# Who makes the low parts of the gated outputs, and when the split of the next weights runs, in a two-block transformer kernel

## What is computed

```python
# first block, layer 0: attention A (windowed), layer 1: attention B
h = h + (o * silu(z)) @ w_out                 # o: attention output, z: gate
gate = sigmoid(rms_norm(h, g) @ ple_w_gate)
h = h + (p @ ple_w) * gate
# second block: a state-space branch and attention C over the same input
y_ssm = ssd_branch(...)
y_att = softmax(q k^T * scale + f_i - f_j, causal) @ v * silu(z_att)
g_ssm, g_att = split(sigmoid(g_logit + b_gate))
merged = g_ssm * (y_ssm @ w_proj_ssm) + g_att * (y_att @ w_proj_att)
x = x + gate * (merged @ w_out)
return rms_norm(x, final_norm_w)
```

## Time and profile before

| | before |
|---|---|
| median of 3 runs | 2878.92 us (2878.53 to 2882.49) |
| the profiled execution's own time | 2878.6 us |
| its span in the trace | 2877.3 us |
| TensorE busy | 2767.1 us, 96% of the span |
| VectorE busy | 1551.6 us, 54% |
| ScalarE busy | 1353.7 us, 47% |
| GpSimd busy | 895.3 us, 31% |
| mean granted TensorE clock | 0.99 of full |
| DMA | 148.78 MB, mean 52 GB/s |

### The profile page before, as it was taken

One profiled execution on the slowest core, in us unless ns is written; L12 is line 12 of the kernel. 1 busy time (PEld: TensorE's weight loads), 2 busy tenths in 40 slices (PEclk: granted clock), 3 DMA queues, 4 the chain that ended last, 5 costly groups with the idle time before them and its releaser, 6 DMA issues.

```text
span 2877.3 us, 36420 instructions
## 1 busy us (share of the span) xinstructions
PE 2767.1 (96%) x13800; PEld 2268.0 (79%) x13800; DVE 1551.6 (54%) x2706; ACT 1353.7 (47%) x2485; POOL 895.3 (31%) x728
## 2 busy tenths in 40 slices
PE   8999989999999999999998999999999999999997
PEld 6778867777788888887775877778787888887875
DVE  6667774643388888886468866521003444433034
ACT  5658864335376766674435344531123334333122
POOL 0334441223365555653122222033221111112331
PEclk9999999999999999999999999999999999999999
DMA  3111131221100000003110310032211010011232
GB/s 132 38 33 41 37 130 64 87 77 44 34 10 10 10 10 10 10 30 132 59 60 28 110 30 19 27 117 73 67 44 37 30 30 30 26 32 47 73 117 73
DMA packets 54444, 148.78 MB, mean 52 GB/s; under 512 B 6144, under 2 KB 14976, under 8 KB 54272
## 3 DMA queue, kind: packets, MB, share of 16 engines
q1 hardware_dynamic: 54272, 146.46, 15.6%
HBM read 129.66 MB, written 16.78 MB: 51 GB/s over the span
## 4 chain that ended last, share of the span: by engine, by line
PE 86%; DVE 5%; ACT 4%; POOL 2%; issue 2%; DMA 0%; SPq 0%; ACTq 0%; POOLq 0%; DVEq 0%
PE ps L327 81%; PE ps L445 4%; PE ps L2656 1%; ACT t L311 1%; PE ps L768 1%; POOL t L318 0%; ACT t L807 0%; POOL t L1308 0%; POOL t L1304 0%; DVE t L898 0%; POOL t L1724 0%; DVE t L3002 0%; DVE t L867 0%; DVE t L2293 0%; DMA t<-in_xT 0%
## 5 line engine op out<-in xcount | busy, mean ns | idle before, releaser
L327 PE MATMUL ps<-t,t 128*128 128x512 f32 (+5 forms) x11912 | 2609.6, 378 | 84.2 <-DVE t L636 8.9
L327 PEld LDWEIGHTS ps<-t,t 128*128 128x128 f32 (+2 forms) x11912 | 2067.4, 185 | 556.3 <-issue 100.9
L318 POOL TENSOR_TENSOR t<-t,t 128x1024 fp32r<-128x1024 f32 (+2 forms) x169 | 362.6, 2146 | 1253.8 <-ACT t L311 1253.0
L311 ACT ACTIVATE t<-t 128x1024 fp32r<-128x1024 f32 (+2 forms) x205 | 187.1, 913 | 656.0 <-PE ps L327 655.4
L1670 DVE TENSOR_TENSOR t<-ps,t 128x512 fp32r<-128x512 f32 x256 | 164.5, 684 | 31.7 <-ACT t L1587 30.1
L1724 POOL TENSOR_SCALAR t<-t,t 128x1024 f32<-128x1024 f32 x128 | 144.1, 1126 | 119.0 <-DVE t L1676 114.0
L445 PE MATMUL ps<-t,t 128*128 128x128 f32 x1176 | 157.2, 274 | 10.5 <-POOL t L1724 7.7
L445 PEld LDWEIGHTS ps<-t,t 128*128 128x128 f32 x1176 | 132.8, 141 | 29.1 <-issue 15.3
L1683 DVE TENSOR_REDUCE t<-ps 128x1 f32<-128x1024 f32 x128 | 154.1, 1204 | 1.8 <-PE ps L327 1.8
L1595 ACT ACTIVATE t<-ps,t 128x1024 f32<-128x1024 f32 x128 | 143.0, 1118 | 2.4 <-DVE t L1683 2.2
L1587 ACT ACTIVATE t<-ps 128x512 fp32r<-128x512 f32 x256 | 139.0, 591 | 8.8 <-PE ps L445 5.0
(11 more groups left out here) (223 smaller groups left out, 2422.3 us busy)
## 6 DMA issues: line engine op xcount, KB each, us to landing
t<-in_wflat SPq DMA_DIRECT2D x156, 512.0 KB, 3.6
t<-in_wada SPq DMA_DIRECT2D x48, 256.0 KB, 4.1
t<-in_xT SPq DMA_DIRECT2D x16, 512.0 KB, 7.3
t<-in_wflat SPq DMA_DIRECT2D x32, 128.0 KB, 2.0
hd<-t SPq DMA_DIRECT2D x8, 512.0 KB, 3.0
t<-hd SPq DMA_DIRECT2D x8, 512.0 KB, 7.5
x2d<-t SPq DMA_DIRECT2D x8, 512.0 KB, 6.6
md<-t SPq DMA_DIRECT2D x16, 256.0 KB, 4.3
```

The lines of the kernel that those rows point to most:

```text
L311: ac.activation(parts(i)[0][:, 0:n], raw[i % 2][:, 0:n], ACT.Copy).then_inc(*on.up(ac, "whi", i))
L318: e.tensor_tensor(lo[:, 0:n], raw[i % 2][:, 0:n], hi[:, 0:n], ALU.subtract) \
L327: return pe.matmul(o, l, r, start=start, stop=stop)
```

## The change

1. In the three places `stage_split_b`, `split_lo` and `merged_lo`, VectorE makes all low parts; GpSimd makes none. At `pa` 7 the addition of the other branch also moves from GpSimd to VectorE, and GpSimd's next weight low part waits until the last of the merged low parts is done.
2. In attention B, three high parts of `OG` are made at step 128 and three at step 130 by ScalarE, two low parts at step 129 and two at step 131 by VectorE. So that `Uh` and `Ul` may be written that early, the buffers that share their place are laid out anew. What is left waits for TensorE's last instruction of attention B alone, no more for GpSimd's; each high part still waits for the gated output that it reads.
3. In attention C, `w_hi` of the block after next no longer stands ahead of the second half's copy out of PSUM but in the step that follows, behind the exponential. GpSimd's `w_lo` for these blocks also waits for a VectorE scaling of that step (`c probs_dv`).

```diff
@@ -1284,11 +1284,15 @@
         R = region(UO)
-        Qs = [(R([P, T], F32R), R([P, T], F32R)) for _ in range(2)]
+        Qs = [(R([P, T], F32R), R([P, T], F32R))]
+        qtab = R([P, T])
         VV = R([P, 8, 2, P], F32R)
-        PT = [(R([P, 8, 256], F32R), R([P, 8, 256], F32R)) for _ in range(2)]
-        qtab = R([P, T])
+        PT = [[R([P, 8, 256], F32R)]]
         Pm.append(R([P, T]))
+        Qs.append((R([P, T], F32R), R([P, T], F32R)))
+        PT[0].append(R([P, 8, 256], F32R))
+        PT.append((R([P, 8, 256], F32R), R([P, 8, 256], F32R)))
         need_cq = lambda k, hf: [("cq_hi", k, hf), ("cq_lo" if k < 2 else "cq_lo_po", k, hf)]
@@ -1466,6 +1470,18 @@
+        EARLY_OG = {NI: 0, NI + 2: 1}
+        og_order_b = [(k, hf) for hf in range(2) for k in range(8)]
+        def og_hi(k, hf):
+            on.wait_ge(ac, "b og_po", 4 * (2 * k + 1) + 2 * hf + 1)
+            ac.activation(Uh[:, k, half(hf)], OG[:, k, half(hf)], ACT.Copy).then_inc(*on.up(ac, "uh", "P", k, hf))
+        def og_lo(k, hf):
+            on.wait_ge(dv, "b og_po", 4 * (2 * k + 1) + 2 * hf + 1)
+            on.wait_ge(dv, "uh", "P", k, hf)
+            dv.tensor_tensor(Ul[:, k, half(hf)], OG[:, k, half(hf)], Uh[:, k, half(hf)], ALU.subtract).then_inc(*on.up(dv, "ul", "P", k, hf))
@@ -1604,6 +1620,12 @@
                         head_ac(*head_step[i])
+                    if i in EARLY_OG:
+                        for k in range(3):
+                            on.wait_ge(ac, "b scores", NI - 9)
+                            if k == 2:
+                                on.wait_ge(ac, "rope", "q", B_HEADS - 1, 1, 1)
+                            og_hi(k, EARLY_OG[i])
                 on.ends(ac, "end attn B", "ac")
@@ -1692,6 +1714,10 @@
                         head_dv(*head_step[i])
+                    if i - 1 in EARLY_OG:
+                        for k in range(2):
+                            on.wait_ge(dv, "b scores", NI - 1)
+                            og_lo(k, EARLY_OG[i - 1])
                 on.ends(dv, "end attn B", "dv")
@@ -1779,31 +1805,20 @@
         def stage_split_b():
-            order = [(k, hf) for hf in range(2) for k in range(8)]
-            def ready(e, k, hf):
-                after(e, "end attn B")
-                on.wait_ge(e, "b og_po", 4 * (2 * k + 1) + 2 * hf + 1)
-            for k, hf in order:
-                ready(ac, k, hf)
-                ac.activation(Uh[:, k, half(hf)], OG[:, k, half(hf)], ACT.Copy).then_inc(*on.up(ac, "uh", "P", k, hf))
-            for e in (dv, po):
-                after(e, "end attn B")
-                for k, hf in order:
-                    name = low_of(order, k, hf)
-                    if e is (dv if name == "ul" else po):
-                        on.wait_ge(e, "uh", "P", k, hf)
-                        e.tensor_tensor(Ul[:, k, half(hf)], OG[:, k, half(hf)], Uh[:, k, half(hf)], ALU.subtract).then_inc(*on.up(e, name, "P", k, hf))
+            for e in (ac, dv):
+                after(e, "end attn B", of=("pe",))
+            for k, hf in og_order_b:
+                if k > 2:
+                    og_hi(k, hf)
+                if k > 1:
+                    og_lo(k, hf)
             on.ends(dv, "end og B", "dv")
             on.ends(ac, "end og B", "ac")
-            on.ends(po, "end og B", "po")
-            return order
-        order_b = stage_split_b()
-        stage_out("G1", BLK["bo"], lambda k, hf: [("uh", "P", k, hf), (low_of(order_b, k, hf), "P", k, hf)], "pn1",
+        stage_split_b()
+        stage_out("G1", BLK["bo"], lambda k, hf: [("uh", "P", k, hf), ("ul", "P", k, hf)], "pn1",
                   (lambda k: hd[k], [("end attn B", ALL)], [("hd", 7)]),
-                  [("end attn B", ALL), ("end og B", ("dv", "ac", "po"))], 1, {})
+                  [("end attn B", ALL), ("end og B", ("dv", "ac"))], 1, {})
         last_row = stage_ple(1, "G1", "D")
@@ -2684,6 +2699,9 @@
                     head_ac(0, s)
+                    if s in (0, 2):
+                        w_hi(parts[s][0][0] + 2)
+                w_hi(FV[0] + 2)
                 for i in range(NF + 4):
@@ -2700,6 +2718,11 @@
                             .then_inc(*on.up(ac, "c exp", i - 1))
+                    if i and head_step(i - 1) and (i - 1) % 8 in (1, 3, 5):
+                        w_hi(parts[(i - 1) % 8][0][(i - 1) // 8 + 1] + 2)
+                    if i in (NF - 6, NF - 4):
+                        w_hi(GA[(i - NF + 6) // 2] + 2)
                     if i < NF and i % 8 in (3, 4):
@@ -2710,8 +2733,6 @@
                         n, hf = divmod(i - NF + 8, 2)
-                        if hf:
-                            w_hi(GA[n] + 2)
                         on.wait_ge(ac, "mm", GA[n], hf)
@@ -2734,8 +2755,6 @@
                     W, hf = parts[s]
-                    if hf:
-                        w_hi(W[h] + 2)
                     on.wait_ge(ac, "mm", W[h], hf)
@@ -2825,8 +2844,14 @@
+            beside = {W[h]: 8 * (h - 1) + x for h in range(1, 8) for W, x in ((FQ, 1), (FK, 3), (FV, 5))}
+            beside.update({GA[0]: NF - 7, GA[1]: NF - 5})
                 for i in each_block():
+                    if i in beside:
+                        on.wait_ge(po, "c probs_dv", beside[i])
                     w_lo(po, i + 2)
@@ -2847,13 +2872,18 @@
+            def merged(n, hf):
+                return ("merged", n, hf) if n < 7 else ("att", 8, hf)
                     for hf in range(2):
-                        users.append(((n, hf), ("merged", n, hf)))
+                        users.append(((n, hf), merged(n, hf)))
             T_ = tmps(users)
-            need_o = lambda k, hf: [("uh", "A2", k, hf), (low_of(order_o, k, hf), "A2", k, hf)]
+            need_o = lambda k, hf: [("uh", "A2", k, hf), ("ul", "A2", k, hf)]
             for e, others in ((dv, ("pe", "ac")), (ac, ("pe", "dv")), (po, ("pe", "dv", "ac")), (sp, ("pe", "dv", "ac"))):
@@ -2897,54 +2927,51 @@
                 on.wait_ge(ac, "U free C", "pe")
-                on.wait_ge(ac, "merged", k, hf)
+                on.wait_ge(ac, *merged(k, hf))
                 ac.activation(Uh[:, k, half(hf)], OG[:, k, half(hf)], ACT.Copy).then_inc(*on.up(ac, "uh", "M", k, hf))
-            def merged_lo(e, k, hf):
-                name = low_of(order_m, k, hf)
-                if e is (dv if name == "ul" else po):
-                    on.wait_ge(e, "uh", "M", k, hf)
-                    e.tensor_tensor(Ul[:, k, half(hf)], OG[:, k, half(hf)], Uh[:, k, half(hf)], ALU.subtract).then_inc(*on.up(e, name, "M", k, hf))
-            def split_lo(e):
+            def merged_lo(k, hf):
+                on.wait_ge(dv, "uh", "M", k, hf)
+                dv.tensor_tensor(Ul[:, k, half(hf)], OG[:, k, half(hf)], Uh[:, k, half(hf)], ALU.subtract).then_inc(*on.up(dv, "ul", "M", k, hf))
+            def split_lo():
                 for k, hf in order_o:
-                    name = low_of(order_o, k, hf)
-                    if e is (dv if name == "ul" else po):
-                        on.wait_ge(e, "uh", "A2", k, hf)
-                        e.tensor_tensor(OS[1][:, k, half(hf)], OG[:, k, half(hf)], OS[0][:, k, half(hf)], ALU.subtract).then_inc(*on.up(e, name, "A2", k, hf))
+                    on.wait_ge(dv, "uh", "A2", k, hf)
+                    dv.tensor_tensor(OS[1][:, k, half(hf)], OG[:, k, half(hf)], OS[0][:, k, half(hf)], ALU.subtract).then_inc(*on.up(dv, "ul", "A2", k, hf))
             def vector():
-                split_lo(dv)
+                split_lo()
                 for nm, n, i in todo:
                         for k, hf in order_m[:14]:
-                            merged_lo(dv, k, hf)
+                            merged_lo(k, hf)
                     for hf in range(2):
                             dv.tensor_tensor(to, ps[:, bank[i, hf], :], to, ALU.mult).then_inc(*on.up(dv, "att", n, hf))
+                            if n == 7:
+                                og = OG[:, n, half(hf)]
+                                on.wait_ge(dv, "att", n, hf)
+                                on.wait_ge(dv, f"{'xm'[hf]}{n}", "merged ssm")
+                                dv.tensor_tensor(og, og, to, ALU.add).then_inc(*on.up(dv, "att", 8, hf))
                 for k, hf in order_m[14:]:
-                    merged_lo(dv, k, hf)
+                    merged_lo(k, hf)
                 on.ends(dv, "end merge", "dv")
             def gpsimd():
-                split_lo(po)
                 for nm, n, i in todo:
-                    if (nm, n) == ("pa", 7):
-                        for k, hf in order_m[:14]:
-                            merged_lo(po, k, hf)
                     for hf in range(2):
                         if hf:
+                            if (nm, n) == ("pa", 7):
+                                on.wait_ge(po, "ul", "M", 7, 1)
                             w_lo(po, i + 2)
-                        if nm == "pa":
+                        if nm == "pa" and n < 7:
                             to = OG[:, n, half(hf)]
```

(6 more changed lines are left out.)

## The result

The changed kernel takes 2861.18 us (median of 4 runs, 2859.14 to 2863.88), the kernel before 2880.09 on the same chip (4 runs, 2878.53 to 2882.49): a ratio of 0.9932, with an interval of 0.9921 to 0.9944. The medians are 18.9 us apart.

The account below looks back on a forecast made before the run. TensorE, busy in 96% of the span, was taken as the bound, so only its waits could yield time. Six terms gave 16.5 us and the clock 0.5: 2878.6 - 17.0 = 2861.6 us, range 2857 to 2867.5.

Parts of the forecast that it names:

- Part 1: End of attention B and the split behind it: early high and low parts gain 1.6 us, before the clock.
- The detour: End of attention B: early copies and low parts ahead of block 127's make TensorE's last product 2.2 us late.
- the clock's loss: End of attention B: a fall of the clock costs between 0 and 1.7 us, taken as 0.9.
- The rival for this part: End of attention B: the early copies cost more than they give, ending at -1.5 us, total 2865.2; chance 0.15.
- Part 2: Wait ahead of attention C's first step: forget gate's copies come earlier, gaining 1.0 us, plus 1.4 for the clock.
- Part 3: Wait in each head of attention C: moving the weight's high part ends seven waits, gaining 6.9 us.
- Nothing is late: Heads of attention C: GpSimd's weight low part comes 2 to 4 us later, but TensorE needs it two steps later.
- Part 4: Step 60: the second low part of v can start at 2586.9 us, gaining 0.6 us.
- Part 5: Start of the merge: VectorE makes GpSimd's low parts too, removing TensorE's wait of 3.5 us; called the safest term.
- Part 6: End of the merge: VectorE's low parts and `pa` 7 additions finish before TensorE asks, gaining 2.9 us.
- the sum: Whole kernel: the six places' 16.5 us and 0.5 for the clock make a gain of 17.0 us.

Follow-up runs that it names:

- e3: Changed kernel with attention C's weight high parts back ahead of the second half's copy and GpSimd's low parts not waiting for the scaling: 2870.95 us, ratio 0.9975.
- e6: Changed kernel with the two additions of `pa` 7 back on GpSimd, its weight still behind VectorE's last low part: 2858.79 us, one run.
- e1: Changed kernel without early copies: all high and low parts behind attention B's block 127, VectorE alone making the low ones: 2859.07 us, ratio 0.9929.
- e2: Changed kernel with six high and four low parts early, but behind block 127's copies and low parts: 2857.73 us, ratio 0.9923.
- e7: Changed kernel with a semaphore wait carried by each of VectorE's sixteen subtractions at the merge's start: 2859.62 us, one run.
- e11: Changed kernel with GpSimd's weight low part at the merge's start made in two instructions of 512: 2865.43 us, one run.
- e4: Changed kernel with only GpSimd's wait for VectorE's scaling removed from its weight low parts in attention C: 2868.41 us, ratio 0.9962.
- e5: Changed kernel with four of the sixteen low parts at the merge's start back on GpSimd: 2868.16 us, one run.

## Why the prediction was right, step by step

**Part 1, the end of attention B: the mechanism right, the size off by the clock.** The detour made the last product late by 2.1 us (2.65 in the times of the two traces, less the 0.55 from before), where it was counted at 2.2, and one wait at k = 2 followed. The term that was mis-sized is the clock's loss, set at 0.9 between 0 and 1.7. Two traces of the same code, e3 and e6, have no fall there; e6's timeline:

```profile
1310.05 3.50 PE L327 MATMUL ps<-t,t 128*128 128x256 f32 x22 [2.88 <-DVE t L1692]
1315.62 11.66 PE L327 MATMUL ps<-t,t 128*128 128x512 f32 x49 [2.07 <-DVE t L1484]
```

The stretch is 30.43 us, a gain of 1.8 where I had 1.6, and the wait at k = 2 is the 2.0 that was forecast. In the profiled run the clock fell at 1311.4, while TensorE stood still behind block 127's transposes; the product and 6 matmuls took 5.92 us instead of 3.5, the last sum and with it VectorE's 14 low parts moved to 1317.55, and the loss was 1.7 (32.11 - 30.43), the upper bound, which came in this trace alone. So 1.6 less 0.9 became 1.8 less 1.7. In the other five traces the clock fell for half as long and the gain was 0.7 to 1.2. The rival for this part (-1.5 us) is not what happened in total, but its core holds: e1 shows that the early copies cost more than they give, by 1.7 us without a fall.

**Part 2, the first step of attention C: right.** The wait went from 3.0 to 2.0 us. For the clock I took 1.4 between 0 and 2.9; it gave 2.6. That 2.6 isn't shown to be the change's: in four of the ten other traces with the wait of 2.0 us (e1, e2, e7, e11) the clock did fall here for 3.4 us, at a cost of about 1.5, and in e3, where the wait is 3.0 us as before, it did not fall. What the shorter wait gives for sure is the 1.0 (12.48 us in e3 for the same matmuls, 10436 to 10480, 11.47 after).

**Part 3, the heads: the number right, one step wrong.** 7.05 us against 6.9. The step that failed is the cost of GpSimd's new wait. The prediction read it as a delay of 2 to 4 us that nobody feels ("Nothing is late") and gave the whole gain to the moved high part. e4 shows the reverse: the moved high part makes GpSimd's low part start where VectorE scales the probabilities, and unless GpSimd waits, the scaling takes 2.71 us for 0.62 and TensorE waits 1.13 us until the earlier transposes' low part has left PSUM. The gain of one wait would have been given back in another. (Without the new wait e4 still has 0.6 to 0.9 of it.) I had counted GpSimd's holding up of VectorE for subtractions only the earlier trace rows, and hadn't asked what VectorE does at the place to which the low part moves.

The Trainium skill ("SBUF — State Buffer", "Who interferes with whom") has the rule for it: the two engines share a pair of SBUF ports; a `tensor_scalar` of VectorE can take both pairs, and then whichever engine issued first keeps the shared one for its whole instruction. The traces agree: begun 0.09 us behind GpSimd's 2.39, the scaling ends 2.71 us later, 0.41 behind GpSimd, and it takes 0.62 when GpSimd is made to wait for it. No run here has a scaling that clearly starts first and meets GpSimd under way: in one of e4's 22 meetings it is recorded 0.02 us ahead of GpSimd, and it was the scaling that waited (2.56 us for 256 columns). The same section says that a VectorE instruction with at most one SBUF input is not held up, as long as it doesn't take both pairs. There too the trace agrees; in e4_free_gpsimd's timeline an operation with one input in PSUM, begun while GpSimd works, takes the 0.69 that it takes alone:

```profile
2161.34 0.69 DVE L2835 TENSOR_TENSOR t<-ps,t 128x512 fp32r<-128x512 f32 x1 [5.92 <-ACT t L2770]
...
2160.91 2.38 POOL L318 TENSOR_TENSOR t<-t,t 128x1024 fp32r<-128x1024 f32 x1 [8.81 <-ACT t L311]
```

**Part 4, step 60: right,** 0.74 for 0.6.

**Part 5, the start of the merge: right,** 3.77 for 3.5. The wait disappeared for the reason given. Two side steps were wrong and cost nothing: VectorE had made twelve low parts before, not eleven (the window of the earlier trace rows ends ahead of the twelfth), and the weight beside the row was to hold VectorE up by 2.4 us, but it was the weight that waited. e5 shows that the term was worth more than the wait: where the clock falls behind it, up to 6.2.

**Part 6, the end of the merge: right,** 3.12 for 2.9. e6 shows which of its edits gives it: not the two additions moved (0.06) but that VectorE makes the low parts with no GpSimd beside it. I had counted them together.

**Why the sum came out.** The misses have both signs: 0.6 less at attention B and 1.5 less at places that the diff doesn't touch, 1.2 more of the clock at attention C, 0.8 more in the other terms. The sum is off by 0.1, but its parts by up to 1.5, so that agreement is partly luck; the profiled runs of the same code at attention B alone differ by 1.7.

**What stays open.** Why VectorE and GpSimd take turns in attention B's split (1.66 us from one to the next in the earlier trace rows) while a row of sixteen at the merge keeps GpSimd out. Neither the size of GpSimd's instruction nor waits carried by VectorE's explain it. The kernel before has the other outcome at the very same place, with twelve subtractions and the same weight:

```profile
2621.94 9.51 DVE L2914 TENSOR_TENSOR t<-t,t 128x512 fp32r<-128x512 f32 x12 [0.17 <-ACT t L2727]
...
2628.19 2.71 POOL L318 TENSOR_TENSOR t<-t,t 128x1024 fp32r<-128x1024 f32 x1 [12.52 <-ACT t L311]
```

GpSimd starts 0.22 us into the eleventh subtraction and gets its turn behind it, and the twelfth takes 2.78 us in place of 0.68; e5 shows the same. After the change it starts 0.22 us into the eleventh as well, and gets no turn. What differs in the rows, besides the length, is that the held twelfth is recorded 0.02 us behind the end of the eleventh, whereas in the row of sixteen each begins some 0.08 us ahead of the end of the one before. Whether that is the reason or what comes of it wasn't tested. Whether the clock falls behind a given wait could not be steered: after waits of 3.5 us it fell in e5 and not in the kernel before.

## What to carry to other kernels

When work is moved off a critical engine, look up what its followers on the other engines land beside: here a GpSimd instruction that became free at a new moment stretched a VectorE scaling from 0.62 to 2.71 us and gave back over 6 of the 7 us, until it was held by a wait that costs nothing. Splitting a row of two-operand subtractions between VectorE and GpSimd lost 2.5 us against VectorE alone. Work done early is only free if it stands behind the last thing that the critical engine waits for: early copies cost 1.7 us ahead of it, more where the clock fell, and gave 1.6 behind it.
